# The first pair of experts gathered in two halves of 64 token places, the second behind the second block of the first expert's gate and up

## What is computed

```python
logits = (xt @ w_router + b_router).astype(jnp.float32)
top_val, top_idx = lax.top_k(logits, MOE_TOPK)
gates = jax.nn.softmax(top_val, axis=-1)
...
def expert_block(args):
    xb, e = args
    gu = xb @ w_gate_up[e] + b_gate_up[e]
    gate, up = gu[:, :MOE_FF], gu[:, MOE_FF:]
    gate = jnp.minimum(gate, SWIGLU_LIMIT)
    up = jnp.clip(up, -SWIGLU_LIMIT, SWIGLU_LIMIT)
    act = (up + 1.0) * (gate * jax.nn.sigmoid(SWIGLU_ALPHA * gate))
    return act @ w_down[e] + b_down[e]
```

## Time and profile before

| | |
|---|---|
| median of 3 runs | 1219.63 us (1215.86 to 1221.7) |
| the profiled execution | 1219.17 us; its span in the profile 1216.8 us |
| TensorE busy | 1128.8 us, 93% of the span |
| VectorE, ScalarE, GpSimd busy | 30%, 15%, 10% |
| mean granted clock of TensorE | 0.981 |
| DMA | 464.68 MB, mean 382 GB/s |
| experts begin | near 304 us |

### The profile page before, as it was taken

How to read it: one execution, slowest core, us unless ns; L and a number is a source line. 1 busy time by engine, 2 the same in 40 slices (tenths; PEclk the granted TensorE clock), 3 DMA queues, 4 the chain that set the end, 5 groups by cost and what they waited for, 6 DMA issues and landing times.

```text
span 1216.8 us, 14754 instructions
## 1 busy us (share of the span) xinstructions
PE 1128.8 (93%) x6181; PEld 583.3 (48%) x6181; DVE 361.9 (30%) x690; ACT 185.3 (15%) x317; POOL 116.0 (10%) x50
## 2 busy tenths in 40 slices
PE   5998999999999999998989899899989999999897
PEld 2898899887443334333333333343324344333332
DVE  1677567352322121221221212122121223122112
ACT  2465444103100000000000000000000010000002
POOL 0775544020000000000000000000000000000000
PEclk9998999999999999999999899999989999999999
DMA  9987535498999999999999999999999999999995
GB/s 353 354 279 236 180 105 209 155 403 342 399 402 428 429 430 430 430 431 430 430 435 432 432 431 431 431 431 431 431 425 430 430 434 434 431 431 429 424 428 241
DMA packets 54513, 464.68 MB, mean 382 GB/s; under 512 B 7087, under 2 KB 29992, under 8 KB 33486
## 3 DMA queue, kind: packets, MB, share of 16 engines
q1 hardware_dynamic: 53644, 462.91, 91.9%
q10 hardware_dynamic: 786, 1.14, 0.3%
q0 software_dynamic: 48, 0.13, 0.0%
HBM read 463.13 MB, written 1.05 MB: 381 GB/s over the span
## 4 chain that ended last, share of the span: by engine, by line
PE 61%; DMA 32%; issue 2%; ACT 2%; POOL 1%; DVE 1%; SPq 0%; DVEq 0%; ACTq 0%
PE ps L511 59%; DMA ring<-in_w_down_dram 20%; DMA ring<-in_w_gate_up_dram 6%; DMA kept<-in_w_down_dram 3%; DMA ring<-in_w_ada_dram 2%; POOL w_lo L1857 1%; PE ps L979 1%; ACT kept L1330 1%; DMA ring<-in_w_in_dram 1%; ACT w_hi L1136 1%; PE ps L1011 0%; SPq L351 0%; DVE kept L1477 0%; PE ps L878 0%; SPq L389 0%
## 5 line engine op out<-in xcount | busy, mean ns | idle before, releaser
L511 PE MATMUL ps<-ring,kept 128*64 128x512 f32 (+2 forms) x2928 | 645.9, 601 | 31.4 <-DMA ring<-in_w_down_dram 20.4
L511 PEld LDWEIGHTS ps<-ring,kept 128*64 128x64 f32 (+2 forms) x2928 | 209.3, 139 | 442.0 <-issue 397.4
L511 PE MATMUL ps<-kept 128*128 128x128 f32 (+5 forms) x952 | 191.6, 419 | 7.7 <-ACT kept L1330 3.3
L511 PEld LDWEIGHTS ps<-kept 128*128 128x128 f32 (+2 forms) x952 | 106.3, 178 | 95.2 <-issue 82.8
L1759 DVE TENSOR_SCALAR kept<-ps 128x512 f32<-128x512 f32 x32 | 22.1, 692 | 379.1 <-PE ps L511 379.1
L1781 DVE TENSOR_TENSOR kept<-ps,kept 64x512 f32<-64x512 f32 x64 | 44.1, 689 | 298.1 <-PE ps L511 297.1
L1326 ACT ACTIVATE kept<-kept 128x512 f32<-128x512 f32 x32 | 20.2, 630 | 728.3 <-DVE kept L1759 728.3
L1857 POOL TENSOR_TENSOR w_lo<-ring,w_hi 128x1024 fp32r<-128x1024 f32 x38 | 101.8, 2698 | 97.0 <-ACT w_hi L1136 97.0
L511 PE MATMUL ps<-hT_hi,w_hi 128*128 128x256 f32 x272 | 78.7, 289 | 1.8 <-POOL w_lo L1857 1.8
L511 PE MATMUL ps<-hT_lo,w_hi 128*128 128x256 f32 x272 | 76.8, 282 | 0.0
L511 PE MATMUL ps<-hT_hi,w_lo 128*128 128x256 f32 x272 | 76.8, 282 | 0.0
(11 more groups left out here) (233 smaller groups left out, 553.0 us busy)
## 6 DMA issues: line engine op xcount, KB each, us to landing
ring<-in_w_gate_up_dram SPq DMA_DIRECT2D x54, 4096.0 KB, 27.9
ring<-in_w_down_dram SPq DMA_DIRECT2D x47, 2048.0 KB, 23.6
ring<-in_w_gate_up_dram SPq DMA_DIRECT2D x19, 2048.0 KB, 21.4
kept<-in_w_down_dram SPq DMA_DIRECT2D x16, 2048.0 KB, 25.1
ring<-in_w_ada_dram SPq DMA_DIRECT2D x24, 1024.0 KB, 7.3
ring<-in_w_in_dram SPq DMA_DIRECT2D x22, 1024.0 KB, 8.5
ring<-in_w_out_dram SPq DMA_DIRECT2D x4, 1024.0 KB, 13.2
ring<-in_w_o_fox_dram SPq DMA_DIRECT2D x2, 1024.0 KB, 6.0
```

Source lines behind the costliest of these rows:

```text
L511: return pe.matmul(dst, lhsT, rhs, start=start, stop=stop, skip_group_check=True)
```

## The change

The gather of the first pair is cut into two, one for each expert of the pair. `gather_early(0)` makes the 64 columns of the first expert with all 16 matmuls and asks only for its half of `onehot`; `gather_early(1)` makes the other 64 columns with 16 more, and stands inside the first expert's `gate_up`, ahead of k = 2. ACT and DVE take each half as it is there. The later pairs are as before. Besides, eleven semaphores of the early part of the layer are merged into two counters, `decay_steps` (DVE's) and `decay_acts` (ACT's).

```diff
+            def gather_early(par):
+
+                pe.wait_ge(S("onehot_early") if par == 0 else S("onehot_ready"), 1)
+                for half in range(2):
+                    b = 7 - half
+                    if par == 1:
+                        pe.wait_ge(S("xg_early_high" if half else "xg_early"), 1)
+                    for kk in range(4):
+                        k = 4 * half + kk
+                        for t in range(TT):
+                            last = mm(bank(b, kk * P + 64 * par, 64), h2tok[:, t, k * P:(k + 1) * P],
+                                      onehot[:, t, 64 * par:64 * par + 64], t == 0, t == TT - 1)
+                    last.then_inc(S("xg_ps" if par else "xg_early_ps"), 1)
+
...
                 for k in range(KD):
-                    if first and k == 4:
+                    if opening and k == 2:
+                        gather_early(1)
+                    if first and not opening and k == 4:
                         pe.wait_ge(S("xg_high_ready"), i + 1)
                     if opening and k == 6:
+                        pe.wait_ge(S("xg_ready"), 1)
                         open_transposes()
...
-                gather(I0 + 1)
+                if isinstance(q, int):
+                    gather_early(0)
+                else:
+                    gather(I0 + 1)
                 pe.wait_ge(S("slots_taken"), 1)
                 gate_up_bias(I0, 0)
-                pe.wait_ge(S("xg_ready"), I0 + 1)
+                if isinstance(q, int):
+                    pe.wait_ge(S("xg_early"), 1)
+                else:
+                    pe.wait_ge(S("xg_ready"), I0 + 1)
...
+            def take_xg_early(par):
+                act.wait_ge(S("xg_ps" if par else "xg_early_ps"), 1)
+                for k in range(4):
+                    last = A(xg[:, k, 64 * par:64 * par + 64], bank(7, k * P + 64 * par, 64), ACT.Identity,
+                             scale=A2_runs[:, k:k + 1], bias=B2_runs[:, k:k + 1])
+                last.then_inc(S("xg_ready" if par else "xg_early"), 1)
+
...
+            def take_xg_early(par):
+                dve.wait_ge(S("xg_ps" if par else "xg_early_ps"), 2)
+                for k in range(4, KD):
+                    last = TS(xg[:, k, 64 * par:64 * par + 64], bank(6, (k - 4) * P + 64 * par, 64), A2_runs[:, k:k + 1],
+                              B2_runs[:, k:k + 1], ALU.mult, ALU.add)
+                last.then_inc(S("xg_high_ready" if par else "xg_early_high"), 1)
...
-                build(onehot, 0, False).then_inc(S("onehot_ready"), 1)
+                if first:
+                    build(onehot, 0, False, range(1)).then_inc(S("onehot_early"), 1)
+                    build(onehot, 0, False, range(1, 2)).then_inc(S("onehot_ready"), 1)
+                else:
+                    build(onehot, 0, False).then_inc(S("onehot_ready"), 1)
...
-                take_xg(I0 * 2 + 2)
                 if first:
+                    take_xg_early(0)
+                    take_xg_early(1)
                     weigh_choices()
+                else:
+                    take_xg(I0 * 2 + 2)
```

More of the change, by code:

```diff
@@ L672, in _ @@
             pe.wait_ge(S("early_in"), 16)
-            pe.wait_ge(S("g8_ready"), 1)
+            pe.wait_ge(S("decay_steps"), 4)
             for t in range(TT):
@@ L679, in _ @@
             mm(bank(2, 328, 8), km("ones"), g8[:, 0, :], False, True).then_inc(S("cums_ps"), 1)
-            pe.wait_ge(S("gb_ready"), 1)
+            pe.wait_ge(S("decay_steps"), 5)
             for h in range(H):
@@ L711, in _ @@
             pe.wait_ge(S("dec_ready"), 1)
-            pe.wait_ge(S("exg_ready"), 1)
+            pe.wait_ge(S("decay_acts"), 4)
             for t in range(TT):
@@ L1048, in pair @@
                 scat_transposes()
+                if opening:
+                    pe.wait_ge(S("xg_high_ready"), 1)
                 gate_up(i, 1, halves_before=0 if opening else None)
@@ L1182, in _ @@
             take("fqk", 0)
-            act.wait_ge(S("s12_ready"), 1)
-            A(beta, s12[:, :, 0:4], ACT.Sigmoid).then_inc(S("beta_ready"), 1)
+            act.wait_ge(S("decay_steps"), 1)
+            A(beta, s12[:, :, 0:4], ACT.Sigmoid).then_inc(S("decay_acts"), 1)
             for u in range(3, 5):
@@ L1188, in _ @@
             link(silu_qkv(5))
-            act.wait_ge(S("y8_ready"), 1)
+            act.wait_ge(S("decay_steps"), 2)
             A(ea, alog_b, ACT.Exp)
-            A(e8, ab8, ACT.Exp, scale=-1.0).then_inc(S("e8_ready"), 1)
+            A(e8, ab8, ACT.Exp, scale=-1.0).then_inc(S("decay_acts"), 1)
             take("fqk", 1)
-            act.wait_ge(S("u8_ready"), 1)
-            A(l8, u8, ACT.Ln).then_inc(S("l8_ready"), 1)
+            act.wait_ge(S("decay_steps"), 3)
+            A(l8, u8, ACT.Ln).then_inc(S("decay_acts"), 1)
             for half in range(2):
@@ L1202, in _ @@
             link(A(exg.rearrange("p (b h) n -> p b (h n)", b=2), ps[:, 3:5, :], ACT.Exp))
-            A(eg, exg[:, :, CH - 1:T:CH], ACT.Copy).then_inc(S("exg_ready"), 1)
+            A(eg, exg[:, :, CH - 1:T:CH], ACT.Copy).then_inc(S("decay_acts"), 1)
             take("fqk", 3)
@@ L1218, in _ @@
             link(A(bx, cums[:, 0, :, 0:H], ACT.Exp))
-            A(kdf, cums[:, 1, :, 0:H], ACT.Exp).then_inc(S("bx_ready"), 1)
+            A(kdf, cums[:, 1, :, 0:H], ACT.Exp).then_inc(S("decay_acts"), 1)
             act.wait_ge(S("dec_ready"), 1)
             A(dec_l, dec_l, ACT.Exp, scale=-1.0)
-            A(dec_a, dec_a, ACT.Exp).then_inc(S("decay_ready"), 1)
+            A(dec_a, dec_a, ACT.Exp).then_inc(S("decay_acts"), 1)
             take("z", 0)
@@ L1330, in expert @@
                 A(act_t_last if par == 0 and not more else act_t, bank(7), ACT.Copy).then_inc(S("act_t_ready"), 1)
+            def take_xg_early(par):
[4 more added lines that the diff above has]
+                last.then_inc(S("xg_ready" if par else "xg_early"), 1)
             def one_round(q):
                 I0 = q * PAIRS
-                take_xg(I0 * 2 + 1)
+                if isinstance(q, int):
+                    take_xg_early(0)
+                    take_xg_early(1)
+                else:
+                    take_xg(I0 * 2 + 1)
                 for par in range(2):
@@ L1459, in _ @@
             ins = CP(s12, bank(2, 256, 24).rearrange("p (t c) -> p t c", t=TT))
-            ins.then_inc(S("s12_ready"), 1)
-            dve.wait_ge(S("s12_ready"), 1)
+            ins.then_inc(S("decay_steps"), 1)
+            dve.wait_ge(S("decay_steps"), 1)
             dve.wait_ge(S("narrow_in"), 80)
@@ L1465, in _ @@
                      ALU.mult, ALU.subtract))
-            STT(ab8, y8, -1.0, y8, ALU.mult, ALU.max).then_inc(S("y8_ready"), 1)
-            dve.wait_ge(S("e8_ready"), 1)
+            STT(ab8, y8, -1.0, y8, ALU.mult, ALU.max).then_inc(S("decay_steps"), 1)
+            dve.wait_ge(S("decay_acts"), 2)
             ins = TS(u8, e8, 1.0, None, ALU.add)
-            ins.then_inc(S("u8_ready"), 1)
-            dve.wait_ge(S("u8_ready"), 1)
+            ins.then_inc(S("decay_steps"), 1)
+            dve.wait_ge(S("decay_steps"), 3)
             link(STT(ab8, u8, 1.0, e8, ALU.subtract, ALU.subtract))
@@ L1475, in _ @@
             link(STT(y8, y8, 0.0, g8, ALU.max, ALU.subtract))
-            dve.wait_ge(S("l8_ready"), 1)
+            dve.wait_ge(S("decay_acts"), 3)
             link(TTn(y8, y8, l8, ALU.add))
@@ L1479, in _ @@
             ins = TS(g8[:, :, 4:8], y8[:, :, 4:8], -1.0, None, ALU.mult)
-            ins.then_inc(S("g8_ready"), 1)
-            dve.wait_ge(S("g8_ready"), 1)
-            CP(gb, g8.unsqueeze(3).to_broadcast([P, TT, 2 * H, P])).then_inc(S("gb_ready"), 1)
+            ins.then_inc(S("decay_steps"), 1)
+            dve.wait_ge(S("decay_steps"), 4)
+            CP(gb, g8.unsqueeze(3).to_broadcast([P, TT, 2 * H, P])).then_inc(S("decay_steps"), 1)
             dve.wait_ge(S("cums_ps"), 1)
@@ L1517, in _ @@
             last.then_inc(S("dec_ready"), 1)
-            dve.wait_ge(S("exg_ready"), 1)
-            dve.wait_ge(S("bx_ready"), 1)
-            dve.wait_ge(S("beta_ready"), 1)
+            dve.wait_ge(S("decay_acts"), 4)
+            dve.wait_ge(S("decay_acts"), 5)
+            dve.wait_ge(S("decay_acts"), 1)
             link(TTn(bx, bx, beta, ALU.mult))
@@ L1539, in _ @@
             dve.wait_ge(S("pairs_ps"), 1)
-            dve.wait_ge(S("decay_ready"), 1)
+            dve.wait_ge(S("decay_acts"), 6)
             for t in range(TT):
@@ L1725, in weigh_choices, with build @@
                 TTn(ypair, ypair, gt2_row, ALU.mult).then_inc(S("bdown_ready"), 1)
-            def build(dst, i, weigh):
-                for par in range(2):
+            def build(dst, i, weigh, pars=range(2)):
+                for par in pars:
                     for t in range(TT):
```

## The result

The changed kernel took 1222.3 us as the median of 9 runs (1221.0 to 1227.6), the kernel before 1217.5 us (1215.9 to 1221.7, 9 runs, the three shown ahead among them). The ratio is 1.0044, interval 1.0031 to 1.0057, so 5.4 us slower, 3.8 to 6.9. The direction and the range held; the forecast of +3.4 us was too small. That 1222.3 lies only 0.7 us from the forecast of 1223.0 is luck: the median of the three runs shown ahead, on which that figure stands, was 2.2 us above the median of all nine, and this hid the 2 us that the sum lacked. The profiled execution took 1223.05 us with a span of 1220.9, 4.1 more than before.

What follows compares the result with a forecast made beforehand. Bound: the down-weight stream, with TensorE's delays before 344 us passing in full. Start -0.49, second half +3.84, seams +0.1 make +3.4 us: 1222.6 profiled, 1223.0 us as median; range 1218 to 1226.5.

Steps and rivals of the forecast that it cites:

- The start: First gather waits for two onehot operations instead of four, so TensorE starts near 304.32 us: gain 0.49 us.
- What bounds the end: Down-weight stream at 430 GB/s bounds the last 800 us; a TensorE delay ahead of 344 us reaches the end in full.
- the stream is unbroken from 344.36 us on: From the issue behind TensorE's fourth block of the second expert, weight transfers were taken to follow without loss.
- The price of a record: In the gather, a record of 64 moved columns costs 0.12 us at full clock; 32 more cost 3.84 us.
- Half price: Rival: a 64-column gather record costs 0.06 us at full clock; -0.2 us, 1219.5 us in all; chance 0.10.
- If the fall comes at the same moment, the first half ends 0.49 us before the old gather did and is no shorter: First half of the gather: 3.4 us at the lower clock as before, so only the 0.49 us earlier start shows.
- a clock of 0.50 past 309.3: Sign against the forecast: TensorE still at half clock after 309.3 us, when the old gather was back at full clock.
- Gate and up at 310.14, k = 0 and 1 in 3.43 us: First expert's blocks after the first half: start at 310.14 instead of 310.63 us, first two done at 313.57.
- the lower clock lasts: Rival: 1.2 GHz until the second half is through, +11.7 us; milder, 3.4 us longer, +1.7; chance 0.12, 0.06 beyond the bound.
- the fall at 94 us: Evidence against a longer low clock: an earlier drop, 94.2 to 97.6 us, ended after as long with work going on.
- the small records at 168 us: Evidence against a longer low clock: 66 small TensorE records in the 2 us from 168 ran at clock 1.00.
- ACT and DVE: Hand-over of gathered columns: ACT done by 308.6 us, DVE by 311.2, both before TensorE asks; cost nothing.

Runs made afterwards that it cites:

- the kernel with doubled columns: The changed kernel, but each matmul of the first half moves its 64 columns twice; ratio 1.0011 to the kernel before, +1.3 us.
- its delay of 16 records: The kernel before, with 16 extra records of 128 columns between k = 1 and k = 2; ratio 1.0018 to the kernel before, +2.2 us.

## Why the prediction was right, and where it was short

- *The start*: -0.49 predicted, -0.45 measured.
- *What bounds the end*: held in the main. The issue at the fourth block of the second expert is where the stream gets its last push; behind it the changed kernel runs at 430 GB/s as before, and TensorE's delay, longer than thought, arrives at the end in all but about 1 us. "In full" was too much said: in every trace with a later issue the landings moved 0.4 to 1.4 us less. The step that was off is "the stream is unbroken from 344.36 us on" read as if that issue alone set the landing; it still stood 4.2 us behind its forerunner, and from issue to landing it took 14.7 us, against 13.3 to 14.2 in the traces where it came later. The chain now turns to down weights at 534 us in place of 474.
- *The price of a record*: held, to 0.12 us, at 3.72 us for the second half and its seams against 3.94. Half price is out.
- *"If the fall comes at the same moment, the first half ends 0.49 us before the old gather did and is no shorter"*: this step failed. The first half and the bias took 1.75 us more. The fall came 1.1 us after onehot in place of 2.2, but what cost was its length. The forecast took the length of the fall from the old gather as if it belonged to the place in the program; it depends on what TensorE runs in it. Among the signs that would make it wrong the prediction names "a clock of 0.50 past 309.3"; it showed, up to 314.5.
- *Gate and up at 310.14, k = 0 and 1 in 3.43 us*: 311.43 and 5.10 us, 1.67 more, for the same reason.
- *The rival "the lower clock lasts"*, in its milder form (one more stretch, +1.7 us), had 0.12 with the long form. It is what happens in every trace of the changed kernel: one more stretch in one, two more in the other. With it the sum is 3.4 + 1.7 = 5.1 and 3.4 + 3.4 = 6.8 us, and the issues at the fourth block moved by 5.0 and 6.7; the landings by 3.8 and 5.6, and the times by 4.9 and 5.4. That the time stayed under the 6.1 us at which the long form was to change the verdict owes something to the 1.1 us hidden in the queue, which the prediction did not have either: two errors of opposite sign. I argued against it with the fall at 94 us and the small records at 168 us. The first ran on with 128 moved columns, the second never had a fall to come back from: neither row was of the case in question.
- *ACT and DVE*: covered, as said. ACT was done at 308.45 for a demand at 311.4, the weights of the choices at 322.82 for transposes at 327.26.
- *The semaphores*: nothing, as said.

## What to carry to other kernels

Cutting a float32 matmul's moved columns did not make it cheaper: with 128 columns of weights, 8, 64 and 128 moved columns all cost 0.12 us a record, so a gather cut in two is a gather done twice. That the weight load sets this pace fits all three, but no run changed the weights. Price such a piece at both clocks, and ask what TensorE runs right behind an idle stretch, since here that set how long the lower clock lasted. And where a stream of weights bounds the end, look for the last issue at which it ran dry: what moves it by more than its wait in the queue moves the end. Take that wait (here up to 1.4 us) off first.

## What the runs showed of the hardware that I had not expected

The granted clock, once down, came back after 3.4 us in seven traces in which TensorE ran records of 128 moved columns, and after 6.8, 10.2 and 17.1 us when it ran records of 64; with the idle time filled ahead of them, 64 records of 64 columns ran at 1.00. The program alone does not decide whether the fall comes: the kernel with doubled columns had it in one trace and not in the other, and of the kernel before and its delay of 16 records, the same up to that point, the first had it and the second did not. Moving each column twice, work of no use, made the changed kernel about 4 us faster.
